# Feed-forward output half of a two-layer decoder step: its first two runs as seven block products instead of eight, with the token sums of the gated product formed tile by tile

## What is computed

```python
def rmsnorm(x, g):
    xf = x.astype(jnp.float32)
    r = lax.rsqrt(jnp.mean(xf * xf, axis=-1, keepdims=True) + EPS)
    return (xf * r * g.astype(jnp.float32)).astype(x.dtype)

def swiglu_ffn(h, w_in, w_out):
    g, u = jnp.split(h @ w_in, [D_FF], axis=-1)
    return (jax.nn.silu(g) * u) @ w_out

# in reference(), for each layer i, prompt and sample tokens alike:
        yp = yp + swiglu_ffn(rmsnorm(yp, norm_ffn[i]), w_ffn_in[i], w_ffn_out[i])
        ys = ys + swiglu_ffn(rmsnorm(ys, norm_ffn[i]), w_ffn_in[i], w_ffn_out[i])
```

## Time and profile before

| | |
|---|---|
| median of 3 runs | 1303.29 us (1303.15 to 1303.53) |
| profiled execution, its own time | 1302.98 us |
| its span, first to last instruction | 1301.2 us |
| mean granted clock of TensorE | 0.991 of full speed |
| busy share of the span | PE 97%, DVE 65%, ACT 41%, POOL 38% |

### The profile page before, as it was taken

One profiled execution on the slowest core, in us unless ns is written; L12 is line 12 of the kernel. 1 busy time (PEld: TensorE's weight loads), 2 busy tenths in 40 slices (PEclk: granted clock), 3 DMA queues, 4 the chain that ended last, 5 costly groups with the idle time before them and its releaser, 6 DMA issues.

```text
span 1301.2 us, 23232 instructions
## 1 busy us (share of the span) xinstructions
PE 1264.8 (97%) x9444; PEld 1219.0 (94%) x9444; DVE 840.7 (65%) x1359; ACT 533.8 (41%) x950; POOL 488.0 (38%) x252
## 2 busy tenths in 40 slices
PE   9999999899999999999999999899999999999997
PEld 8888899899999999998889999799999999999996
DVE  5766757982288516858447778678981388428754
ACT  5565645452155414543023354224452255315531
POOL 1000034343344333446565544275333444334440
PEclk9999999999999999999999999899999999999998
DMA  9411111132122222233232333123223222222222
GB/s 325 159 34 50 50 66 66 65 98 98 65 98 98 98 82 82 98 98 115 81 104 80 122 126 109 62 66 114 68 96 98 65 97 98 97 65 98 98 82 73
DMA packets 37610, 121.83 MB, mean 94 GB/s; under 512 B 5649, under 2 KB 9681, under 8 KB 36065
## 3 DMA queue, kind: packets, MB, share of 16 engines
q1 hardware_dynamic: 33680, 107.01, 24.9%
q10 hardware_dynamic: 3824, 13.34, 2.8%
HBM read 112.86 MB, written 9.44 MB: 94 GB/s over the span
## 4 chain that ended last, share of the span: by engine, by line
PE 88%; issue 4%; DVE 4%; ACT 2%; POOL 2%; DMA 1%; SPq 0%; POOLq 0%; ACTq 0%; DVEq 0%
PE ps L662 28%; PE ps L664 27%; PE ps L663 27%; POOL wlo L612 1%; PE ps L791 1%; PE ps L838 1%; PE ps L814 1%; PE ps L1120 1%; ACT whi L2085 1%; PE ps L1127 1%; DMA wst<-w_blocks_in 1%; DVE S L1831 1%; DVE acc L1254 1%; DVE ring_sum L1513 0%; PE ps L1111 0%
## 5 line engine op out<-in xcount | busy, mean ns | idle before, releaser
L612 POOL TENSOR_TENSOR wlo<-wst,whi 128x1024 fp32r<-128x1024 f32 x101 | 252.0, 2495 | 357.7 <-ACT whi L2085 354.9
L662 PE MATMUL ps<-hid,whi 128*128 128x288 f32 x704 | 209.8, 298 | 3.8 <-POOL wlo L612 2.9
L662 PE MATMUL ps<-xhi,whi 128*128 128x288 f32 x688 | 208.6, 303 | 1.1 <-DVE wlo L1330 0.7
L663 PE MATMUL ps<-hid,whi 128*128 128x288 f32 x704 | 209.0, 297 | 0.0
L664 PE MATMUL ps<-hid,wlo 128*128 128x288 f32 x704 | 208.7, 296 | 0.0
L663 PE MATMUL ps<-xlo,whi 128*128 128x288 f32 x688 | 202.9, 295 | 0.0
L664 PE MATMUL ps<-xhi,wlo 128*128 128x288 f32 x688 | 202.3, 294 | 0.0
L621 POOL TENSOR_TENSOR wlo<-wst,whi 128x512 fp32r<-128x512 f32 x72 | 105.1, 1463 | 202.8 <-ACT whi L2147 202.8
L2085 ACT ACTIVATE whi<-wst 128x1024 fp32r<-128x1024 f32 x66 | 69.9, 1059 | 170.7 <-PE ps L664 170.7
L662 PEld LDWEIGHTS ps<-hid,whi 128*128 128x128 f32 x704 | 133.3, 189 | 5.7 <-POOL wlo L612 4.3
L662 PEld LDWEIGHTS ps<-xhi,whi 128*128 128x128 f32 x688 | 128.9, 187 | 9.6 <-issue 8.3
(11 more groups left out here) (279 smaller groups left out, 3063.7 us busy)
## 6 DMA issues: line engine op xcount, KB each, us to landing
wst<-w_blocks_in SPq DMA_DIRECT2D x188, 512.0 KB, 3.5
S<-s_in ACTq DMA_DIRECT2D x4, 1024.0 KB, 4.9
s_sample_out<-S ACTq DMA_DIRECT2D x4, 1024.0 KB, 4.3
bias<-bias_in SPq DMA_DIRECT2D x1, 2048.0 KB, 11.1
y_out<-x SPq DMA_DIRECT2D x14, 144.0 KB, 1.8
x<-x_in SPq DMA_DIRECT2D x4, 288.0 KB, 6.8
x<-x_in ACTq DMA_DIRECT2D x4, 288.0 KB, 6.5
ktx<-ktx_in SPq DMA_DIRECT2D x1, 1024.0 KB, 12.8
```

What stands on the lines that cost most here:

```text
L612: nc.gpsimd.tensor_tensor(wlo[:, n % RING, :], wst[:, slot, :], raw(whi[:, n % RING, :]), ALU.subtract).then_inc(w_split, 1)
L662: mm(out, stat[0], mov[0], start=start, stop=False, skip_group_check=skip)
L663: mm(out, stat[0], mov[1], start=False, stop=False, skip_group_check=skip)
```

## The change

The output half of the first two runs becomes units as well. Two output tiles (2i and 2i+1) by two halves of the run's eight hidden tiles make the 2 x 2 block of weights, the two halves of the hidden tiles by two halves of the tokens the other one, and four output units ("out", ph, 0) to ("out", ph, 3) follow each of the first two runs in one list, `UNITS`. Each has the same seven products, weight sums, high parts and low parts as an input unit. The third run keeps `down` as before, but its last output tile in layer 1 has only this run's 36 matmuls left in `last_down`.

The token operands of the output half are formed as the hidden tiles come. Tiles 0 to 3 of a run (`first_half`) give B11 (left half of the tokens) and T1 (right minus left). Tiles 4 to 7 give B21 and B22 (both halves) and, together with tile f - 4, T2, T3 and T4. DVE forms the sums (`hidden_sum`), ACT the high parts (`sum_high`), POOL the low parts (`hidden_low` on POOL). POOL also takes the low parts of T3 and T4 of the input half over from DVE.

The core of the diff:

```diff
+UNITS = ([("in", f) for f in range(N_DIRECT, 8)] + [("out", 0, i) for i in range(4)] +
+         [("in", f) for f in range(8, 16)] + [("out", 1, i) for i in range(4)] + [("in", f) for f in range(16, FC)])
...
+            def hidden_low(l, op, f):
+
+                j = f % 4
+                pool.wait_ge(ht_hi[op], turn_of(l, f))
+                if op == "T2":
+                    pool.wait_ge(ht_lo["T1"], turn_of(l, f))
+                nc.gpsimd.tensor_tensor(htlo[op][:, j, :], htraw[op][:, j, :], raw(hthi[op][:, j, :]), ALU.subtract
+                                        ).then_inc(ht_lo[op], 1)
...
+                prev = None
+                for u, nxt in zip(UNITS, UNITS[1:] + [None]):
+                    quarter_low("A11", l, nxt)
+                    if in_halves(prev) and not first_half(prev[1]):
+                        hidden_low(l, "T2", prev[1])
+                        hidden_low(l, "T3", prev[1])
+                    quarter_low("A22", l, u)
+                    if in_halves(prev) and first_half(prev[1]):
+                        hidden_low(l, "T1", prev[1])
+                    quarter_low("A12", l, nxt)
+                    if in_halves(prev) and not first_half(prev[1]):
+                        hidden_low(l, "T4", prev[1])
+                    prev = u
...
                     for c in range(4):
+                        if u[0] == "out" and u[2] == 0:
+                            f = PHASES[u[1]][0] + c
+                            if op[0] == "B":
+                                pe.wait_ge(h_lo[l], f + 1 + (4 if op != "B11" else 0))
+                            else:
+                                pe.wait_ge(ht_lo[op], turn_of(l, f))
...
+                    product(6, "S2", "T2", u, a, False)
+                    if u[0] == "in":
+                        product(2, "A12", "B21", u, 6, True)
                     pe.wait_ge(copied[5], o)
-                    product(3, "S4", "B22", f, 7, False)
+                    product(3, "S4", "B22", u, 7, False)
+                    if u[0] == "out":
+                        product(2, "A12", "B21", u, 6, True)
...
+                before = None
+                for u in UNITS:
+                    seven(u, before)
+                    before = u
+                n_in = PHASES[2][1] - PHASES[2][0]
+                down(0, 0, 3)
+                left_up(before)
+                down(0, 3, n_in - 1)
+                down(1, 0, n_in - 1)
+                down(0, n_in - 1, n_in)
+                down(1, n_in - 1, n_in)
+                for m in range(2, KC - l):
+                    down(m, 0, n_in)
...
+                    xl, xr = x[:, 2 * u[2], 0:H], x[:, 2 * u[2], H:N]
+                    dve.wait_ge(copied[1], o)
+                    chain.link(tt(xl, xl, kept[:, 0, :], ALU.add))
+                    dve.wait_ge(copied[6], o)
+                    chain.link(tt(xr, xr, kept[:, 2, :], ALU.add))
                     dve.wait_ge(product_done[2], o)
+                    tt(xl, ps[:, 6, 0:H], xl, ALU.add).then_inc(top_read, 1)
...
+                    ins = tt(out, h32[:, H:N], gs[:, H:N], ALU.mult)
+                    if in_halves(u) and not first_half(f):
+                        chain.link(ins)
+                        hidden_sum("T2", f)
+                        hidden_sum("T3", f)
...
+                    sum_low("S1", nxt)
+                    if in_halves(prev) and not first_half(prev[1]):
+                        hidden_sum("T4", prev[1])
+                    top(u)
```

More of the change, by code:

```diff
@@ L1576, in down @@
-                def down(ph, m):
-                    dve.wait_ge(*used(DOWN_AT[l][ph][m]))
-                    if ph:
-                        dve.wait_ge(*added(l, ph - 1, m))
-                    tt(cols(x, m), pair(2 * (m % 2)), cols(x, m), ALU.add).then_inc(added(l, ph, m)[0], 1)
-                    if ph == 2:
-                        prepare(k + 1, m, m == 0)
+                    dve.wait_ge(corner_read, ordinal(l, u))
+                    out = htraw["T3"][:, f % 4, :] if in_halves(u) and first_half(f) else h32[:, H:N]
```

625 lines of the change are left out of this document (331 added, 294 removed).

## The result

| | median | ratio to before, 95% interval | span profiled | granted clock |
|---|---|---|---|---|
| before | 1303.41 us | | 1301.2 us | 0.991 |
| changed | 1337.72 us | 1.0263 [1.0248, 1.0278] | 1334.8 us | 0.981 |

What follows compares the result with a forecast made beforehand. TensorE's matmul stream bounds the kernel (97% busy), with DVE and POOL excluding each other in T units. Span: 1301.2 - 25.5 - 4.6 - 0.9 + 2.1 + 44 = 1316.3 us; forecast time 1318 us, range 1288 to 1331.

Steps and rivals of the forecast that it cites:

- Matmuls: 16 output units take 84 matmuls instead of 96: 192 fewer at 0.133 us, 25.5 us less.
- Seams: TensorE's waits of 0.48 and 0.68 us around a run's output vanish, four times each: 4.6 us less.
- The T tiles: Units with a run's second-half hidden tiles: 13.3 us each, 2.1 over TensorE; with output units and tiles 8-11, 44 us more.
- the layout of 13.5 us: A T unit's DVE and POOL operations laid out in program order, excluding each other: 13.5 us, the upper bound.
- The first output unit: First output unit after a run: tile 7's subtractions and a dependence at product 6 make it 16.0 us, 4.6 over.
- The sign that I named: In units 5 to 7 and 13 to 15, TensorE would wait for DVE's right up half (L1676).
- The rivals with less exclusion: Cover down to the exclusive work, 1301 or 1295 us (chance 0.22); no binding exclusion, 1274 us (chance 0.13).
- The first units: Start of each layer's units: A11's earlier low part against POOL's added exclusion, counted 0, bounds -3 to +4 us a layer.
- The third run: The new order of down covers the 0.46 us wait for the last hidden tile: 0.9 us less over two layers.
- The tail: Layer 1's end: 48 matmuls fewer, but they hid the first token half's norm; 4.3 us shorter, 2.1 given back.
- Time beside the span: Median over the profiled span: 1.8 us plus 0.3, taking the span of 1316.3 us to 1318.4.
- The worse rival: First units cost their 4 us, ACT is late or slow-clock stretches come: above 1330 us, 1341 named; chance 0.10.

Runs made afterwards that it cites:

- narrow: Probe on the changed kernel: POOL's low parts of T1 to T4 of the hidden tiles cover 8 of 288 columns, result incomplete; 1316.55 us.
- copy_first: Changed kernel with ACT's copy of product 1 issued ahead of the high parts of T2 and T3 instead of behind them; 1345.15 us.
- fixes_dve_quarters: fixes_dve with POOL's low parts of A22 and the next unit's A12 moved to DVE in units behind a T tile; 1302.10 us.
- no_pool_early: all_dve with POOL's last low part (A11) on DVE too, behind the gate halves, in units behind a T tile alone; 1302.30 us.
- first_units: Changed kernel with the feed-forward's first phase reordered: small T1 and T3 operations behind POOL's splits and ACT's late split and SiLU; 1328.61 us.
- operands_dve: Changed kernel with the low parts of token operands T3 and T4 (1152 columns each) back on DVE instead of POOL; 1332.04 us.
- all_dve: fixes_dve_quarters with the low parts of token operands T3 and T4 back on DVE; 1298.13 us, ratio 0.9961 to the kernel before.
- old_down: Changed kernel with the third run's block 1 of the second down projection multiplied wholly after block 0, as before the change; 1330.21 us.
- narrow_copy: Probe joining narrow and copy_first on the changed kernel, result incomplete; 1316.67 us.
- fixes_dve: Changed kernel with old_down, first_units and the low parts of the hidden tiles' T1 to T4 on DVE instead of POOL; 1312.01 us.

## Why the prediction was off, point by point

**Matmuls.** Right: 25.5 us less, and units without T work take 11.15 to 11.18 us.

**Seams.** Mis-sized: I counted TensorE's idle time in the earlier trace rows, 1.16 us for two, but the interval around a `down` was 1.8 to 1.9 us over its matmuls, 7.4 us for four instead of 4.6.

**The T tiles.** The mechanism is right: narrow, copy_first and fixes_dve_quarters each move the time as turns between DVE and POOL ask for. The size is 39.0 where I had 44. A T unit is 1.4 over, not 2.1, because the layout of 13.5 us held for a DVE without a pause, and the pause for product 6 covers part of POOL's A11. copy_first takes the pause away and measures 13.46. The first output unit and the one behind it are 5.0 over together, where I had put 4.6 on the first alone. The sign that I named, waits for the right up half, was wrong: TensorE waits 0.74 us for copy 1. The rivals with less exclusion are refuted. That all low parts on DVE would end the excess is refuted too: no_pool_early has such a unit at 12.16 us with POOL idle.

**The first units.** This is the step that failed. "I count 0, bounds -3 to +4 for each layer" measured +9.1 and +7.5. I had balanced A11's earlier low part against the exclusion by the two operands and stopped there. Two things were missing. The small T1 operations were put into ACT's and POOL's queues ahead of work that TensorE waits for: its splits come 2.98 and 2.03 us late in layer 0, 1.76 and 2.04 in layer 1, and first_units wins 9.1 us. And POOL's two low parts of 1152 columns don't only take 2.7 us each from a sum over DVE, but hold one certain sum for 3.06 us, behind which the first S4 high part, copy 1, TensorE and some 4 us at the 1.2 GHz level stand in a row; operands_dve wins 5.7. In all_dve, with both cured, the second S2 sum starts at 265.04, 2.2 us after the kernel before, and layer 1's stretch to it is 394.3 us against 393.7. So all but 2.8 of the 16.6 us are gone with these two (all_dve also has T1's low parts on DVE); the 2.8 stay open. The added sums and low parts are the likely rest, but no run isolates them.

**The third run.** "Their wait of 0.46 us is covered by the new order of `down`" was true and beside the point. I looked at the wait that the new order covers and not at the ring slot it holds: block 0's last part comes behind most of block 1, its slot is free later, POOL's split of block 2 starts later, and TensorE waits 2.84 us, with a half-clock stretch behind the wait. Forecast 0.9 us less, measured 7.9 more. old_down shows it.

**The tail.** Right in the main: from the last tile's first matmul to the second half's token sums it is 11.84 us (1312.61 to 1324.45) against 15.99 before, 4.15 less where I had 4.3. The half-clock stretch is 3.5 us long, about as before (3.3 in the earlier trace rows). Another 0.5 us is lost behind the token sums, so 2.7 us are given back and not 2.1; no run isolates the 0.5.

**Time beside the span.** 2.9 us, not 2.1, between median and span: the profiled execution is the fastest of four, 1.1 us under the median.

The size of the miss is thus the first units (16.6) and the third run (8.8), less what the T units (5.0) and the seams (2.8) came out better. Without the first units' 16.6 us the time would lie inside the range. The worse rival (1341) named the first units' 4 us and ten half-clock stretches for 15 us, and came nearest, but in part by luck: its price of the first units was less than half the true one, the stretches came (six more than before) but are worth at most 7.8 us, and the third run is not in it.

## What to carry to other kernels

Where a change puts small operations into the queues of several engines, walk through the start of the stage instruction by instruction, as for the steady state: ask of each added one what it stands ahead of, and who waits for that. Price an operation on POOL by what it takes from DVE, not by POOL's busy share: a subtraction of 512 float32 columns costs DVE's chain about 1.1 us on POOL, where it meets neither a pause nor a PSUM operation of DVE, and 0.6 on DVE, so that "offloading" it makes a busy DVE slower. Price a wait of TensorE with the half-clock stretch that can follow it: here 2.4 us of wait were 3.8 to 4.0 us of time. And when an engine's pause lies beside another's exclusive work, removing the wait that causes the pause can cost more than it gives; look what the pause covers first.

## What the runs showed of the hardware

- Freeing a copy 0.7 us earlier took away TensorE's wait for it and made the unit 0.8 us longer (12.63 to 13.46), 7.4 us in all.
- A POOL subtraction of 288 columns takes 0.81 us alone, and of 8 columns 0.20 us (in the traces of copy_first and narrow_copy). The first is above the 0.72 of my estimate. DVE has a new start 0.37 us after one of 288 columns.
- The Trainium skill's page Perfetto Trace Analysis, Optimizing Scalar/DVE Operations, warns that moving operations between DVE and GpSimd might not help as they share an SBUF read port. The runs go further: the move to POOL costs, and the move back wins 9.9 us from fixes_dve to fixes_dve_quarters.
- The Trainium skill's GPSIMD Engine Reference, section 3.1 (Elementwise), gives a float32 addition of two tensors of 2048 elements as taking 1.96 times as long on GpSimd as on VectorE. The subtraction of 1152 columns agrees: 2.67 us on POOL and 1.34 on DVE.
